# Moving VectorE and ScalarE work within a triangular inverse: convolution taps, a table load, a decay product, and the order of two groups of matmuls

## What is computed

```python
qkv = silu(causal_conv(concat([q, k, v]), conv_w))     # 4 taps on each channel
q, k, v = split(qkv);  q = l2norm(q) * 64**-0.5;  k = l2norm(k)
g = cumsum(g) within a chunk;  kb = k * beta;  vb = v * beta
lmat = where(strictly_lower, (kb @ k.T) * exp(g_i - g_j), 0)
sol = solve(eye + lmat, concat([vb, kb * exp(g)]))
u_val, w_k = sol[:, :dv], sol[:, dv:]
for each chunk:                       # S is the 64 x 64 state of a head
    v_new = u_val - w_k @ S
    o = (q * exp(g)) @ S + attn @ v_new
    S = S * exp(g_last) + (k * exp(g_last - g)).T @ v_new
```

## Time and profile before

| | us |
|---|---|
| three runs | 1591.36, 1593.31, 1591.96 |
| median | 1591.96 |
| the profiled execution | 1593.14 |
| its span, first to last instruction | 1591.30 |
| what lies around the span | 1.84 |
| PE busy, DVE busy, ACT busy, POOL busy | 1549.6, 1261.4, 925.0, 105.0 |
| the inverse's five rounds, layer 0 | 113 to 139 |
| the same, layer 1 | 525 to 551 |

### The profile page before, as it was taken

How to read it: one execution, slowest core, us unless ns; L and a number is a source line. 1 busy time by engine, 2 the same in 40 slices (tenths; PEclk the granted TensorE clock), 3 DMA queues, 4 the chain that set the end, 5 groups by cost and what they waited for, 6 DMA issues and landing times.

```text
span 1591.3 us, 23022 instructions
## 1 busy us (share of the span) xinstructions
PE 1549.6 (97%) x8860; PEld 1249.0 (78%) x8860; DVE 1261.4 (79%) x1203; ACT 925.0 (58%) x787; POOL 105.0 (7%) x128
## 2 busy tenths in 40 slices
PE   8999999999999899999999999999999999999995
PEld 6767687888787757888888888888888888888874
DVE  6996665444549776888888888888888888888996
ACT  1254153443206424777777777777777777777774
POOL 0011192000000201000000000000000000000200
PEclk9999999999999999999999999999999999999998
DMA  8430578774443115999999999999999999999993
GB/s 326 160 107 29 198 290 307 278 287 174 159 160 122 53 67 196 396 393 395 395 396 361 395 395 346 395 394 348 396 394 347 396 394 347 397 393 356 396 395 136
DMA packets 190452, 472.25 MB, mean 297 GB/s; under 512 B 7632, under 2 KB 11856, under 8 KB 189328
## 3 DMA queue, kind: packets, MB, share of 16 engines
q1 hardware_dynamic: 186352, 454.23, 76.8%
q0 software_dynamic: 3024, 13.42, 2.2%
q10 hardware_dynamic: 1008, 3.67, 0.6%
HBM read 463.43 MB, written 25.69 MB: 307 GB/s over the span
## 4 chain that ended last, share of the span: by engine, by line
PE 85%; DVE 10%; issue 3%; ACT 2%; DMA 1%; ACTq 0%; SPq 0%; DVEq 0%; POOLq 0%
PE ps L1637 45%; PE ps L1648 24%; PE ps L1608 5%; PE ps L2045 4%; PE ps L1710 2%; DVE arena L1052 1%; PE ps L1615 1%; ACT hi L666 1%; DVE lo L1152 1%; DVE arena L1075 1%; DVE arena L1095 1%; DMA arena<-in_w_in 1%; PE ps L1629 0%; PE ps L1949 0%; PE ps L2063 0%
## 5 line engine op out<-in xcount | busy, mean ns | idle before, releaser
L1152 DVE TENSOR_TENSOR lo<-arena,hi 128x2048 fp32r<-128x2048 f32 x378 | 868.3, 2302 | 205.9 <-ACT hi L666 205.0
L666 ACT ACTIVATE hi<-arena 128x2048 fp32r<-128x2048 f32 x378 | 723.5, 1919 | 357.2 <-PE ps L1637 226.9
L1637 PE MATMUL ps<-hi,xg 128*128 128x512 f32 x1760 | 543.6, 390 | 0.6 <-DVE lo L1152 0.2
L1637 PEld LDWEIGHTS ps<-hi,xg 128*128 128x128 f32 x1760 | 329.1, 188 | 71.2 <-DVE lo L1152 3.6
L1637 PE MATMUL ps<-lo,xg 128*128 128x512 f32 x880 | 342.4, 389 | 0.0
L1648 PE MATMUL ps<-hi,hTe 128*128 128x512 f32 x896 | 282.4, 396 | 0.0
L1637 PEld LDWEIGHTS ps<-lo,xg 128*128 128x128 f32 x880 | 165.2, 188 | 34.4
L1648 PEld LDWEIGHTS ps<-hi,hTe 128*128 128x128 f32 x896 | 164.2, 188 | 31.9
L1648 PE MATMUL ps<-lo,hTe 128*128 128x512 f32 x448 | 175.1, 391 | 0.0
L1637 PE MATMUL ps<-hi,xs 128*128 128x512 f32 x512 | 159.8, 393 | 3.2 <-issue 2.1
L1608 PE MATMUL ps<-arena 128*128 128x256 f32 x544 | 121.8, 386 | 2.8 <-DMA arena<-in_w_in 1.8
(11 more groups left out here) (371 smaller groups left out, 1271.0 us busy)
## 6 DMA issues: line engine op xcount, KB each, us to landing
arena<-in_mg SPq DMA_DIRECT2D x112, 1024.0 KB, 7.7
arena<-in_mu SPq DMA_DIRECT2D x112, 1024.0 KB, 8.1
arena<-in_md SPq DMA_DIRECT2D x112, 1024.0 KB, 7.3
arena<-in_w_in SPq DMA_DIRECT2D x7, 2048.0 KB, 9.7
arena<-in_wg SPq DMA_DIRECT2D x14, 1024.0 KB, 5.1
arena<-in_wu SPq DMA_DIRECT2D x14, 1024.0 KB, 5.1
arena<-in_wd SPq DMA_DIRECT2D x14, 1024.0 KB, 5.3
xg_rows<-in_zeros SPq DMA_DIRECT2D x17, 512.0 KB, 7.3
```

Of the source, the lines that this page charges most:

```text
L666: af(hi[r % PARTS][:, :], raw[r % RAWS], ACT.Copy).then_inc(hi_ready, 1)
L1152: tt(lo[r % PARTS][:, :], raw[r % RAWS], hi[r % PARTS][:, :].bitcast(F32), ALU.subtract)\
L1637: ins = mm(ps[:, (4 if w == "G" else 4 + nb) + b, :], tok[a][:, kk * nt + b * P:kk * nt + (b + 1) * P], tiles_of(part[r % PARTS], w)[:, k, ...
```

## The change

Four moves, all within each layer's inverse. No arithmetic is added or dropped.

- The four taps of channel block 7 stood behind groups 0, 0, 1, 2 of round 0. Now all four stand behind group 2 of round 0. Those of block 8, in round 1, stay.
- ACT loads Silu's table after its copy number 6 (round 2, group 0), not after number 7.
- The keys' decay into kg stood behind round 3. Now it stands behind round 4, ahead of the one into kd, and raises a semaphore of its own, kg_ready.
- PE multiplies values and U first and keys and U second, and the second waits for kg_ready.

```diff
+        kg_ready = sem("kg_ready")
...
                     if n in (2, 3, 4):
                         probabilities(2 * n - 4, 2 * n - 3)
+                    if n == 6:
+                        act.preload_act_table_set("silu_and_others")
                     if n == 7:
...
-                            for w in ((0, 1), (2,), (3,))[g]:
+                            for w in (((), (), (0, 1, 2, 3)), ((0, 1), (2,), (3,)))[v][g]:
                                 tap(l, 7 + v, w)
...
-                    if v == 3:
-                        dve.wait_ge(kv_evac, 4 * l + 2)
-                        by_decay(kg, eg)
+                dve.wait_ge(kv_evac, 4 * l + 2)
+                by_decay(kg, eg, kg_ready)
                 by_decay(kd, ekl)
...
+                for b in range(NB):
+                    for h in range(NH):
+                        i = 6 * (h % 2) + 2 * (h // 2) + b
+                        for c in range(2):
+                            rows = chunk_rows(c)
+                            ins = mm(ps[rows, (2, 5)[b], h * HD:(h + 1) * HD], U[rows, i, :],
+                                     kv[rows, 1, b, h * HD:(h + 1) * HD], start=True, stop=True)
+                    ins.then_inc(up_psum_, 1)
+                pe.wait_ge(kg_ready, NB * (l + 1))
                 for jb in range(6):
...
                 ins.then_inc(w_psum, 2)
-                for b in range(NB):
-                    for h in range(NH):
...
-                    ins.then_inc(up_psum_, 1)
```

More of the change, by code:

```diff
@@ L1316, in _, with by_decay @@
                        ALU.subtract).then_inc(u_ready, 1)
-                def by_decay(dst, by):
+                def by_decay(dst, by, ready=None):
                     h4 = "p (j r d) -> p j r d"
                     for b in range(NB):
-                        step(tt(dst[:, b, :].rearrange(h4, j=3, r=2), kv[:, 0, b, :].rearrange(h4, j=3, r=2),
-                                by_bh(by)[:, b].unsqueeze(3).to_broadcast([P, 3, 2, HD]), ALU.mult))
+                        ins = tt(dst[:, b, :].rearrange(h4, j=3, r=2), kv[:, 0, b, :].rearrange(h4, j=3, r=2),
+                                 by_bh(by)[:, b].unsqueeze(3).to_broadcast([P, 3, 2, HD]), ALU.mult)
+                        if ready is not None:
+                            ins.then_inc(ready, 1)
+                        else:
+                            step(ins)
                 for v in range(5):
```

## The result

| | before | after |
|---|---|---|
| median of 22 executions, us | 1592.13 | 1594.47 |
| lowest and highest | 1590.74 to 1594.02 | 1592.65 to 1597.75 |
| ratio of after to before, 95% interval | | 1.0016 (1.001 to 1.0022) |
| the profiled execution | 1593.14 | 1592.92 |
| its span | 1591.30 | 1591.1 |

The time came out where it was forecast. Yet the two profiled spans say that nothing changed: the one of after is 0.2 shorter.

What follows compares the result with a forecast made beforehand. The inverse was taken as bound by a chain of handovers, with no engine full. Per layer 1.36 - 0.08 = +1.28, for two layers +2.56, on the median 1591.96 + 2.56 = 1594.5 us; range 1590.9 to 1596.2.

Steps and rivals of the forecast that it cites:

- The hold by POOL: Round 0: POOL's third mask goes ahead of tap 3 and holds it, delaying round 1's first subtraction by 1.36 us a layer.
- The margin of 0.07: Round 0's taps: the mask was estimated at 120.72, within tap 2 and 0.07 us ahead of tap 3.
- The first rival: Round 0: tap 3 starts ahead of the mask, which holds block 8's tap 0 instead; -0.30 a layer, 1591.4; chance 0.18.
- kg, -0.08: Ahead of round 4: without the decay its third group begins at 138.47, not 138.55; only 0.08 us a layer gained.
- The table load and the order of products: Silu's load fits idle time ahead of ACT's copy 7; values before keys behind round 4 makes nobody wait; 0 each.
- The clock as a rival: TensorE's clock falls in the longer wait ahead of product_a(2, 0): 1596.0 with one layer hit, 1597.5 with both; chance 0.12.
- the shift goes through whole: Behind both mixers, channel mixers' first weights wait in buffers, so the span grows by the inverses' full +2.56 us.

Runs made afterwards that it cites:

- The taps alone: The kernel before with only the four taps of block 7 moved behind round 0's group 2: 1595.16 us, ratio 1.0014 to the kernel before.
- taps_back: The changed kernel with the four taps back at their old places, the other three moves kept: 1592.38 us, ratio 0.999 to the kernel before.
- The forced case: The changed kernel with an unused DVE reduction of 1.75 us added behind the four taps: 1599.87 us, ratio 1.0045 to the kernel before.
- mask_later: The changed kernel with POOL's third mask also waiting for round 1's first subtraction: 1591.01 us, ratio 0.998 to the kernel before; repeated, 1590.72 and 0.9986.
- the filled wait: The changed kernel with 15 unused transposes added on PE ahead of product_a(2, 0): 1594.06 us, ratio 1.0011 to the kernel before.
- the last two traces of the changed kernel: The changed kernel without any edit, one profiled execution each: 1594.87 and 1593.47 us.
- the second measurement: The changed kernel timed once more without any edit: 1594.72 us, ratio 1.0005 to the kernel before.
- three_attention: The changed kernel with block 7's tap 3 behind round 1's group 0 and attention ahead of product_a(2, 0): 1590.2 us, ratio 0.9988; repeated, 1590.18 and 0.9985.

## Why the prediction was right, by its own steps

**The hold by POOL, +1.36 a layer: measured +1.30.** From the first subtraction of round 0 to that of round 1 it was 121.55 - 114.48 = 7.07 and is 122.40 - 114.03 = 8.37. The taps alone gave +1.29 and +1.30 for the whole inverse. Each link stood where the sum had it, if 0.45 is added for after's earlier start. PE's timeline has no idle time ahead of product_a(1, 1) any more, and behind it the transposes:

```profile
118.23 0.87 PE L1903 MATMUL ps<-cst,score_rows 128*128 128x128 f32 x6
```

They are at 118.68 (forecast 118.67), the mask at 120.73 (forecast 120.72), tap 3 at 120.79 (120.79), its length 2.04 (2.08), the subtraction at 122.85 (122.91). The mask ended at 122.53 for 122.59 forecast, and this is the difference of 0.06. Whether POOL waited for tap 2 can't be read here: its record begins 0.02 ahead of that tap's end, but a record can hold waiting, as the prediction itself read it in the earlier trace rows, and 0.02 is near what the trace resolves.

The Trainium skill, SBUF — State Buffer, section Who interferes with whom, says that an instruction of VectorE with two SBUF inputs contends with one of GpSimd that reads SBUF, and that one with at most one SBUF input does not, outside the 2-port perf modes. The traces agree for tap 3 (2.04 instead of 0.50) and for the subtractions (0.42 beside a mask and without one). The prediction left out the exception. It bears on tap 0: its instruction, a TENSOR_SCALAR, has one data tensor, its other operand being one value for each partition, and it too was held (1.12 instead of 0.36). The same section of the Trainium skill names tensor_scalar among those that can enter such a mode; no run here shows the mode itself.

**The margin of 0.07** was thin, and held in all seven traces with the four taps in a row and the mask as it was: the mask came 0.05 ahead of tap 3 each time. The first rival, tap 3 ahead of it, would have been -0.30 a layer; with the mask made later it was -0.31. The price was right; the case did not occur by itself.

**kg, -0.08: measured -0.05 to -0.07** (taps_back). The third group began at 138.49 for 138.47 forecast. **The table load and the order of products, 0:** the load stands in idle time ahead of copy 7, as this timeline of ACT shows (answering), and the key products follow the value products without a gap:

```profile
124.27 1.28 ACT L853 ACT_TABLE_LOAD   x1
...
127.32 0.38 ACT L849 ACTIVATE arena<-ps 128x256 f32<-128x256 f32 x1 [1.77 <-PE ps L1946]
...
128.47 0.84 ACT L856 ACTIVATE arena<-arena 128x768 f32<-128x768 f32 x1 [0.77 <-DVE arena L1055]
```

```profile
140.00 1.55 PE L2026 MATMUL ps<-arena 64*64 64x64 f32 x45 [0.74 <-DVE arena L1347]
141.44 0.87 PE L2035 MATMUL ps<-arena 64*64 64x64 f32 x46
```

Silu waits 0.77 for DVE's last tap, not for its table. In the trace these three moves are worth 0.1 us in the inverses of both layers, while the ratio of taps_back says 0.2 to 3.0; most of that I can't place in the stretches, and it stays open.

**The clock as a rival, 0.12.** It is not in the forecast's sum, and no trace of the changed kernel shows it. Three things speak for its happening in some executions. The forced case: a wait of 4.2 does bring the fall, at 1.7 a layer, near the 1.5 put down. The spread: in after's 22 executions, the 8 with a mean clock of 0.996 or more average 1593.30, the 11 with 0.994 or less 1596.48, 3.2 apart; two falls of 3.4 us at half the clock take 0.002 off the mean over 1591 us, and would cost twice 1.7. In the kernel before (1593.57 for 23 executions at 0.995 or more, 1593.87 for 10 at 0.994 or less) and in mask_later (correlation +0.02) the two hardly go together. And the filled wait has none above 1596.

But the router explains the spread as well. The traces give it 63.0 to 66.0 by its falls alone, a difference of 3.0, and 6.8 us at half the clock there take off the same 0.002. No trace of the changed kernel has that double fall, and none has a fall in the inverse, so no run tells the two apart. The filled wait speaks against the router as the only cause, though its own times still go with the mean clock; and that mean also moves with the end of the span, as the last two traces of the changed kernel show. So a part of the +2.3 us of the median may be the clock's, in the wait or in the router: **argued, not shown**. The forecast of +2.56 names the mechanism seen in every trace; what share the clock has is open.

**What no step foresaw** is the router. The prediction said that the shift goes through whole. In the profiled execution it did not: 1.72 came back where the clock had fallen before and now didn't. The sum had no term for this. The traces give the router stretch 63.0 without a fall, 64.4 to 64.7 with 3.4 us of it, and 66.0 with 6.8. Which it is differs among executions of the same kernel (after 63.01, 63.02, 64.39 and 64.38; the later mask 64.39 and 62.99), so it widens the spread of everything measured here and is no property of the change alone. The step to which it belongs, that the span changes by what the inverses change, was too simple. That the median came out 2.3 up, near the 2.56 forecast, is in part luck: the executions with a full clock are only 1.2 up (0.2 in the second measurement), the long ones much more, and the median lies between. The loss in the inverses, 2.44 for 2.56 forecast, is not luck: it is in every trace, and taps_back lies 2.34 below the changed kernel beside it.

## What to carry to other kernels

Where DVE has a row of instructions with two SBUF operands ahead of one that others wait for, find out when POOL's next one falls due, and arrange the two so that it lands on a filler for which nobody waits. Here making POOL's instruction later took 1.54 off a layer's inverse, and moving one tap behind the subtraction 2.07. Judge such a change by the length of its own stretch, between two fixed instructions, and not by the profiled span, which moves with other things: one fall of TensorE's clock elsewhere is worth 1.4 to 1.7 us here, the start of the first inverse 2.6, and the change 2.44. And when a handover gets faster, look whether the next engine has work to place into the wait that is left, as attention ahead of product_a(2, 0).

## What the runs showed of the hardware that was not expected

- An instruction of POOL that falls due while DVE works through taps which stand 0.04 apart gets in between two of them (its record begins at 120.28, the tap before it ends at 120.30, the next begins at 120.33). The next one of DVE then lasts until 0.28 behind POOL's end. The seven traces with that order agree to 0.01 in both.
- The granted clock can fall while PE counts as busy throughout: at 608 to 611 before, PE is busy all the time, with products of 128x512 at half speed. Just ahead of the fall it works through 32 matmuls of only 8 columns for 3.6 us (from 603.48). After has the same matmuls (from 604.77, 3.6 us) and no fall. The same kernel can have none or 3.4 us of it (after, mask_later), or 3.4 or 6.8 (three_attention). What decides between them no run shows.
- The wait of 2.4 us kept the full clock in ten out of ten inverses traced; the one of 4.2 us lost it in two out of two.
